# Building the expert gate matrix: one-pass products with split gates, sums on VectorE, weight rests on GpSimd

## What is computed

```python
units  = gelu(h @ peer_u.T)              # 256 tokens x 16384 experts, 128 tiles of 128 experts
gates  = sum over a token's slots of gate * onehot(row) x onehot(column)   # 128 x 128 per token
h      = h + (units * gates) @ peer_v    # 128 tiles
```

## Time and profile before

| | before |
|---|---|
| three runs | 1803.19, 1803.84 and 1809.23 us, median 1803.84 |
| profiled execution, first to last instruction (span) | 1795.7 us |
| PE busy | 97% |
| DVE, ACT, POOL busy | 70%, 52%, 27% |
| the 64 turns of `u2` | 776 to 1014 us of the span |
| from 769.7 us on, PE in the chain that ended last | 631.0 us without a break |

### The profile page before, as it was taken

The page is one execution under the profiler, slowest core; times in us unless marked ns, Lnnn a source line. Parts: engine busy times, 40 slices in busy tenths (PEclk is TensorE's granted clock), DMA queues, the critical chain, the costliest instruction groups (busy, mean ns, idle before and its releaser), DMA issues.

```text
span 1795.7 us, 33010 instructions
## 1 busy us (share of the span) xinstructions
PE 1744.2 (97%) x11190; PEld 1547.2 (86%) x11190; DVE 1251.2 (70%) x2359; ACT 942.1 (52%) x1389; POOL 492.9 (27%) x225
## 2 busy tenths in 40 slices
PE   9999989999999999999999999999999999999997
PEld 6799878897878999999999988888888787669996
DVE  4567587876424499067777578888888896667777
ACT  5466577544555544567777643333333575334444
POOL 4246744401568588800000000000000100013332
PEclk9999999999999999999999999999999999999999
DMA  6654443577344478755565687677767783355553
GB/s 216 200 188 141 166 152 118 190 248 266 121 164 150 135 222 228 228 179 172 174 173 173 195 263 239 235 235 236 237 239 236 272 276 122 113 176 187 183 183 113
DMA packets 122839, 347.63 MB, mean 194 GB/s; under 512 B 13904, under 2 KB 46800, under 8 KB 122512
## 3 DMA queue, kind: packets, MB, share of 16 engines
q1 hardware_dynamic: 121248, 339.52, 58.1%
q0 software_dynamic: 1520, 7.21, 1.1%
HBM read 328.84 MB, written 17.83 MB: 193 GB/s over the span
## 4 chain that ended last, share of the span: by engine, by line
PE 84%; DVE 6%; ACT 4%; issue 2%; POOL 2%; DMA 1%; POOLq 0%; DVEq 0%; ACTq 0%
PE banks L934 83%; POOL weight_rest L851 2%; ACT arena L1676 2%; DMA weight_ring<-in_stream 1%; ACT weight_high L1676 1%; PE banks L945 1%; DVE weight_rest L2307 1%; ACT span_exponentials L1676 0%; DVE arena L3110 0%; DVE arena L2991 0%; DVE arena L2348 0%; ACT scratch L1676 0%; ACT L1676 0%; DVE arena L2347 0%; DVE arena L2345 0%
## 5 line engine op out<-in xcount | busy, mean ns | idle before, releaser
L1676 ACT ACTIVATE weight_high<-weight_ring 128x1024 fp32r<-128x1024 f32 x448 | 473.0, 1057 | 453.4 <-PE banks L934 350.4
L851 POOL TENSOR_TENSOR weight_rest<-weight_ring,weight_high 128x1024 fp32r<-128x1024 f32 x165 | 414.4, 2521 | 264.5 <-ACT weight_high L1676 155.0
L2307 DVE TENSOR_TENSOR weight_rest<-weight_ring,weight_high 128x1024 fp32r<-128x1024 f32 x283 | 346.1, 1224 | 156.3 <-ACT weight_high L1676 153.4
L934 PE MATMUL banks<-a_high,weight_high 128*128 128x256 f32 x1216 | 304.0, 288 | 0.2 <-ACT weight_high L1676 0.2
L934 PE MATMUL banks<-a_rest,weight_high 128*128 128x256 f32 x1216 | 297.8, 283 | 0.0
L934 PEld LDWEIGHTS banks<-a_high,weight_high 128*128 128x128 f32 x1216 | 232.6, 191 | 1.5 <-issue 1.1
L934 PEld LDWEIGHTS banks<-a_rest,weight_high 128*128 128x128 f32 x1216 | 232.9, 192 | 0.3 <-issue 0.2
L934 PE MATMUL banks<-weight_high,gated_high 128*128 128x512 f32 x512 | 201.4, 393 | 0.0
L934 PE MATMUL banks<-weight_high,gated_rest 128*128 128x512 f32 x512 | 200.2, 391 | 0.0
L934 PE MATMUL banks<-a_high,weight_rest 128*128 128x256 f32 x1216 | 170.9, 283 | 2.4 <-POOL weight_rest L851 2.4
L934 PE MATMUL banks<-x_high,weight_high 128*128 128x256 f32 x672 | 167.5, 287 | 4.7 <-DVE x_rest L3079 3.7
(11 more groups left out here) (360 smaller groups left out, 3101.5 us busy)
## 6 DMA issues: line engine op xcount, KB each, us to landing
weight_ring<-in_stream SPq DMA_DIRECT2D x512, 512.0 KB, 3.5
arena<-in_stream SPq DMA_DIRECT2D x66, 512.0 KB, 3.3
unit_spill<-small SPq DMA_DIRECT2D x128, 128.0 KB, 3.6
scratch<-unit_spill SPq DMA_DIRECT2D x128, 128.0 KB, 3.2
residual<-in_x SPq DMA_DIRECT2D x2, 512.0 KB, 4.1
arena<-in_mem POOLq DMA_DIRECT2D x2, 512.0 KB, 5.3
arena<-in_ctx POOLq DMA_DIRECT2D x2, 512.0 KB, 4.8
arena<-in_keys POOLq DMA_DIRECT2D x1, 1024.0 KB, 5.2
```

Source lines behind the costliest of these rows:

```text
L851: nc.gpsimd.tensor_tensor(w_lo[:, e % 2, :], raw(e)[0], w_hi[:, e % 2, :], ALU.subtract).then_inc(S["rest_ready"], 1)
L934: return nc.tensor.matmul(out, lhsT, rhs, start=start, stop=stop, skip_group_check=True)
L1676: return nc.scalar.activation(out, in_, f, **kw)
L2307: tt(w_lo[:, e % 2, :], raw(e)[0], w_hi[:, e % 2, :], ALU.subtract).then_inc(S[ready], 1)
```

## The change

A token's product becomes one matmul in the one-pass format. The column one-hots are exact in it. The row one-hots are made twice side by side, times the gate's high part and times its rest, so that the matmul has 256 columns and gives two halves; DVE adds them with a `tensor_reduce` from PSUM into `WT`. Four tokens now fill banks 6 and 7 together, and all four w jobs of a loop turn use this one place. ACT no longer copies the result; it makes the column one-hots of three turns in four. POOL makes the rests of all 128 units tiles. Two slots ahead, DVE makes the row one-hots of the tokens of turn k+2 right behind the sum of turn k. `row_onehots` occupies all of `scratch`, so the first loads of stored units wait for the last product.

```diff
-UD = U0 + 52
+UD = U0 + P
...
-    B.loop("w", T // 16, 4, banks=(6, 7, 6, 7))
-    B.loop("u3", U_LATE // 4, 4, banks=(4, 5, 6, 7))
+    B.loop("w", T // 16, 4, banks=(6, 6, 6, 6))
+    B.loop("u3", U_LATE // 4, 4, banks=(4, 5, 4, 5))
...
+        columns_r = over("column_onehots_one_pass", "column_onehots", 0, [P, 2, 4, P])
+        rowhots = over("row_onehots", "scratch", 0, [P, 2, 4, 2, P])
+        gates_high = over("gates_high", "scratch", 0, [P, T])
...
+        GATE_SUMS = ps[:, 6:8, :].rearrange("p b (v x n) -> p (b v) x n", v=2, x=2)
...
-            with pool.Fori(0, U_EARLY // 4) as i:
+            with pool.Fori(0, P // 4) as i:
                 for j in range(4):
                     split_rest(U0 + j, i, 4)
...
-                        ins = mm(b[:, hsl(v)], COLUMN[:, u % 2, v, :], ROWHOT[:, u % 2, v, :])
+                        ins = mm(GATE_SUMS[:, v], columns_r[:, u % 2, v, :], rowhots[:, u % 2, v])
                     filled(ins, ("w", u))
...
                 split_high(U0 + U_EARLY + u + 2, i, 4)
-                dense(i, u)
+                if u < 3 and more:
+                    arrived(act, ("w", u), i)
+                    columns(i * 16 + (4 * u + 8), u, i * 3 + (u + 2))
...
-            ts(slots[:, 3, :], slots[:, 1, :], -1.0, None, ALU.mult).then_inc(S["slots_negated"], 1)
-            with dve.Fori(0, T // 16) as i:
+            step(cp(gates_high[:, :], slots[:, 2, :]))
+            step(tt(slots[:, 3, :], slots[:, 2, :], gates_high[:, :], ALU.subtract))
+
+            def row_onehots(token, u):
+                for v in range(4):
+                    at = bass.ds(token + v, 1)
+                    ins = stt(rowhots[:, u % 2, v], bc(C("iota"), 1, 2), slots[:, 0, at],
+                              slots[:, 2:4, at].to_broadcast([P, 2, P]), ALU.is_equal, ALU.mult)
+                ins.then_inc(S["onehot_ready"], 1)
...
+            def dense(turn, u):
+                arrived(dve, ("w", u), turn)
+                out = WT[:, :, bass.ds(turn * 16 + 4 * u, 4)].rearrange("p n v -> p v n")
+                free(V.tensor_reduce(out, GATE_SUMS.rearrange("p v x n -> p v n x"), AX.X, ALU.add), ("w", u))
+
+            for u in range(2):
+                row_onehots(4 * u, u)
+            column_quad(4)
+            with dve.Fori(0, T // 16 - 1) as i:
                 for u in range(4):
-                    split_rest(UD + u, "lo_ready", i, 4)
...
-                    for v in range(4):
-                        slot = bass.ds(i * 16 + (4 * u + v), 1)
-                        ins = ts(ROWHOT[:, u % 2, v, :], C("iota"), slots[:, 0, slot], slots[:, 2, slot],
-                                 ALU.is_equal, ALU.mult)
-                    ins.then_inc(S["onehot_ready"], 1)
-                    if u:
-                        quad = bc(slots[:, 1, bass.ds(i * 16 + 4 * u, 4)], 2, P)
-                        tt(COLUMN[:, u % 2], bc(C("iota"), 1, 4), quad, ALU.is_equal).then_inc(S["dve_columns"], 1)
-            with dve.Fori(0, U_LATE // 4) as i:
-                for j in range(4):
-                    split_rest(UD + U_GATED + j, "lo_ready", i, 4)
+                    dense(i, u)
+                    row_onehots(i * 16 + (4 * u + 8), u)
+                    if u == 3:
+                        column_quad(i * 16 + 20)
```

More of the change, by code:

```diff
@@ L548, in build @@
             x1_hi_ready x1_lo_ready x2_hi_ready x2_lo_ready cx_hi_ready cx_lo_ready rest_ready column_ready square_made
[L549 removed]
+            constants_made residual_scaled y_squares y_mean y_root masks_joined log_hi_ready log_lo_ready o_squares epsilon_set gated_made hidden_ready hidden_made summed""".split()
         S = {n: sem(n) for n in names}
@@ L808, in load_units @@
                     sp.wait_ge(S["p_ready"], a - 3)
+                else:
+                    arrived(sp, ("w", 3), T // 16 - 1)
                 sp.dma_start(UNITS_IN[:, a % 4, :], spill[a]).then_inc(h_in[a % 4], 16)
@@ L1384, in _ @@
                 transposes(("eTr", t), [EAB[:, t, x, :] for x in range(3)])
+            for t in range(TT):
+                freed(pe, ("eTr", t))
             pe.wait_ge(S["ctx_kd"], 1)
@@ L1397, in _ @@
                     pe.wait_ge(S["onehot_ready"], i * 4 + (u + 1))
-                    if u == 0:
-                        pe.wait_ge(S["column_ready"], i + 1)
-                    else:
-                        pe.wait_ge(S["dve_columns"], i * 3 + u)
-                    b = claim(("w", u), i)
+                    if u == 1:
+                        pe.wait_ge(S["dve_columns"], i + 1)
+                    else:
+                        pe.wait_ge(S["column_ready"], i * 3 + (1, 0, 2, 3)[u])
+                    claim(("w", u), i)
                     for v in range(4):
-                        ins = mm(b[:, hsl(v)], COLUMN[:, u % 2, v, :], ROWHOT[:, u % 2, v, :])
+                        ins = mm(GATE_SUMS[:, v], columns_r[:, u % 2, v, :], rowhots[:, u % 2, v])
                     filled(ins, ("w", u))
@@ L2053, in _, with columns, unit_and_columns @@
                 evacuate(("cH", d), h0[:, d], src=quarters)
-            act.wait_ge(S["slots_negated"], 1)
-            def columns(turn):
+            for t in range(TT):
+                freed(act, ("eTr", t))
+            def columns(token, u, made):
                 for v in range(4):
-                    ins = func(COLUMN[:, 0, v, :], C("iota"), ACT.Square,
-                               bias=slots[:, 3, bass.ds(turn * 16 + v, 1)])
+                    ins = func(column_onehots[:, u % 2, v, :], C("iota"), ACT.Square, scale=-1.0,
+                               bias=slots[:, 1, bass.ds(token + v, 1)])
                 ins.then_inc(S["square_made"], 1)
[L2062 to L2071, removed]
+                act.wait_ge(S["square_made"], made)
+                func(columns_r[:, u % 2], column_onehots[:, u % 2], ACT.Relu, scale=-1.0, bias=1.0).then_inc(S["column_ready"], 1)
+            columns(0, 0, 1)
+            def unit_and_columns(i, u, more=True):
                 act.wait_ge(h_out[u], i * 16 + 16 * U_EARLY // 4)
@@ L2075, in unit_and_gates @@
                 split_high(U0 + U_EARLY + u + 2, i, 4)
-                dense(i, u)
+                if u < 3 and more:
+                    arrived(act, ("w", u), i)
+                    columns(i * 16 + (4 * u + 8), u, i * 3 + (u + 2))
             with act.Fori(0, T // 16 - 1) as i:
                 for u in range(4):
-                    unit_and_gates(i, u)
-                    if u == 2:
-                        columns(i + 1)
+                    unit_and_columns(i, u)
             for u in range(4):
-                unit_and_gates(T // 16 - 1, u)
+                unit_and_columns(T // 16 - 1, u, u < 2)
             with act.Fori(0, U_LATE // 4) as i:
@@ new lines, in column_quad @@
+            def column_quad(token):
+                quad = bc(slots[:, 1, bass.ds(token, 4)], 2, P)
+                tt(columns_r[:, 1], bc(C("iota"), 1, 4), quad, ALU.is_equal).then_inc(S["dve_columns"], 1)
+            def dense(turn, u):
[4 more added lines that the diff above has]
+                row_onehots(4 * u, u)
@@ L2792, in _ @@
+            column_quad(4)
+            with dve.Fori(0, T // 16 - 1) as i:
+                for u in range(4):
+                    dense(i, u)
+                    row_onehots(i * 16 + (4 * u + 8), u)
+                    if u == 3:
+                        column_quad(i * 16 + 20)
+            for u in range(4):
+                dense(T // 16 - 1, u)
+                if u < 2:
+                    row_onehots(T - 8 + 4 * u, u)
             for u in range(4):
```

4 lines of the change are left out of this document (removed).

## The result

| | before | after |
|---|---|---|
| median, lowest and highest of 4 runs each | 1803.51 (1801.34 to 1809.23) | 1858.13 (1855.71 to 1861.76) |
| profiled execution, span | 1795.7 | 1859.9 |
| mean turn of `u2` (from the first turn's products to the last turn's, 63 steps) | 3.76 | 4.62 |

A forecast was written before the change was run, and what follows sets the result against it. The prediction took DVE to bound u2: sum 1.14 + row operations 1.60 + column 0.15 + wait for POOL 2.22 = 5.11 us per turn against 3.76, +86 us, plus 1 before the loop: 1891 us, range 1810 to 1945.

The forecast's parts named there:

- The sign and the mechanism: Slower, chance 0.86: in u2 the loop closes over DVE, whose row operations wait for POOL, and PE waits for the sum.
- PE's 3.35 us possible: PE in u2: products cost 0.48 us instead of 0.89, a turn of 3.35 us if PE stays the bound.
- The sum: DVE's sum of 1024 elements from PSUM: 1.14 to 1.94 us per turn, taken as 1.14.
- the slow sum: Rival: the reads of DVE's sum are slow, 1.94 us, turn 5.91 us, +138 us, 1942; chance 0.22.
- Four row operations: DVE in u2: 0.40 us each to the next start, 1.60 us per turn (low bound 1.36).
- The column: DVE's column operation in u2: 0.60 us in one turn of four, 0.15 us per turn.
- ACT and `u3` at nothing: ACT's 3.02 us fits a turn of 3.35; moving rests to POOL in u3 costs nothing.
- The price of one rest: Shared path: one POOL rest costs DVE 2.82 - 0.60 = 2.22 us.
- How the two meet: In u2 POOL's rest goes in among DVE's row operations every turn; the last waits 2.22 us, turn 5.11 us, +86 us.
- The packed rival: Rival: the sum always falls into POOL's 2.22 us, 3.97 us per turn, +13 us, 1817; chance 0.14.
- Before the loop: DVE's first operations ahead of u2's loop delay the start: 1 us added (0 to 4).
- The clock: Rival: PE's clock falls to half, 1.2 GHz; tile and products take 6.70 us, +188 us, 1992; chance 0.02.

The follow-up runs named there:

- the products inside the tile: Changed kernel with each turn's four products between the 16 matmuls with weight_high and the 8 with weight_rest of their tile: 1843.65 us.
- halves: Changed kernel with every weight rest of the units made by GpSimd in two subtractions of 512 columns instead of one of 1024: 1840.44 us.
- the kernel with one bank: Changed kernel with DVE's row and column operations reading iota from PSUM bank 5, all u2 tiles using bank 4: 1802.56 us.

## Why the prediction was right, and where it was off

*The sign and the mechanism* were right: DVE is the bound of `u2`, PE waits for its sum, and what makes DVE's turn long is the row operations' wait for POOL's rests. Four kernels show it from three sides: without POOL beside it (rests on DVE) 1817, without the contention but with POOL (iota from PSUM) 1803 and 1787, and with the contention but without DVE's new work 1804.

*The terms.* PE's 3.35 us possible: measured 3.35. The sum, "the term I trust least", 1.14: measured 1.14 to the next start, so the slow sum (0.22) did not come. Four row operations 1.60: measured 1.58. The column 0.15: right. ACT and `u3` at nothing: right. POOL's 2.40 (2.4 to 2.8 in "What would show it"): median 2.41, up to 3.26. The price of one rest, 2.22 us: 2.13 in the timeline above where a rest fell wholly among the row operations, at most 2.21 (the longest row operation, 2683 ns). The row operations, with 256 columns in 473 ns, run at the full rate that the earlier trace rows gave. The Trainium skill (Vector Engine (DVE) Microarchitecture Reference, section 7, Points that are easy to get wrong) has half that rate for a scalar-tensor-tensor with two SBUF sources wider than bf16; here the measurement decides against it.

*The step that failed* is the one under "How the two meet": "DVE is by then in its third row operation. POOL goes in between, the last row operation waits 2.22 us", for every turn. It took each turn to begin with PE waiting for the sum. In the trace PE waits for the sum in 26 of 64 turns only. After a long turn everything for the next is ready, PE passes through it in 3.35 us, and POOL's next rests start by PE's and ACT's pace and not by the sum's end. Then some rests lie partly beside the sum (906.47) and some turns take two (907.27). On average a rest costs DVE 1.69 us and not 2.22: 2.87 + 1.69 = 4.56, with 0.09 of DVE idle near the 4.62 measured, instead of 5.11. That is a size, and it is the whole difference: 64 x 0.49 = 31 us, against 1891 - 1858 = 33. The packed rival (3.97, 0.14) was the other end of this; the truth lies between the two. How far between could be moved by when the rests start (4.31 with eight more matmuls, 4.38 with the products inside the tile, 4.35 with halves), and with the rests on POOL only reading iota from PSUM removed it.

*Before the loop* I had 1 us for DVE's first operations. There were 1.8, for another cause: PE waits ahead of the first products for ACT's evacuation of the stage before, a wait that the change adds and the prediction did not name.

*The clock.* It was priced as all or nothing (0.02, 1992). It fell to 0.89 in `u2`, and where I looked only for part of a tile behind a gap of PE. PE was busy for 167 of 200 us, 84% and not the "near 66%": 3.35 of 4.62 us are 73%, and the slower clock makes the rest. As DVE is the bound (idle for 5.6 us in all of `u2`), a slower tile can cost only by where it puts the rests. The kernel with four more matmuls had the whole clock and saved 13 of the 55 us; how much of these 13 is the clock and how much the later start of the rests stays open.

## What to carry to other kernels

Work moved to GpSimd is not off VectorE's turn: beside a GpSimd subtraction of SBUF tensors, VectorE's operations on tensors that all lie in SBUF waited in these kernels, up to 2.2 us for one of 2.40. Such a wait shows as a long operation with no idle time, so compare the median of a group with its mean. It costs nothing where VectorE has that much room in its turn (before: yes; with 1.3 us more work in the turn: no), so before adding work to either, add to VectorE's turn what the rests take from it (here 1.1 to 2.1 us of each 2.4). If it doesn't fit, put one operand of VectorE's operations in PSUM; if that can't be, cut GpSimd's instructions shorter or start them where VectorE reads PSUM.

## What the runs showed of the hardware that was not expected

- *One operand in PSUM is enough.* Row and column operations with iota in PSUM and the gates or slots in SBUF (as pointer scalars, and as a broadcast operand) never waited beside POOL's 2.40 us: in the kernel with one bank all 256 row operations took at most 484 ns. The Trainium skill (GPSIMD Engine Reference, section 8, Key points) names operations with two SBUF inputs and those in a 2-port mode, and these runs agree.
- *An operation with one SBUF tensor and pointer scalars waits too.* In the kernel before with POOL's rests the row one-hots are of that kind, and their mean rose from 341 to 859 ns. The prediction had a row of one-tensor kind that waited (481.93), but gave two SBUF tensors as the condition. The Trainium skill (GPSIMD Engine Reference, section 8, Key points) has besides these only operations in a 2-port mode; no row here shows an operation's mode.
- *POOL holds the path for one instruction.* VectorE's wait was 2.13 to 2.21 us, when a rest fell wholly among row operations, for a subtraction of 1024 columns (2.40 us) and 1.04 for one of 512 (1.28 us where it did not wait itself). The Trainium skill (SBUF — State Buffer, Terms) calls the shared port pair exclusive and held for the full instruction; the two prices agree with it.
- *The granted clock fell for parts of a tile.* In the window 800 to 1000 us it was 0.89 in the changed kernel with PE busy for 167 us, 0.96 with products inside the tile and the same 167, 0.94 with the rests in halves and 168, and 1.00 with four more matmuls and 179. Busy time alone does not order these four. PE's longest waits before its products were 2.63, 3.69, 2.65 and 1.13 us in them; these runs give no rule.
